# A first feed-forward pass in plain products, and Strassen's seven products on normalised rows, added up in one PSUM bank

## What is computed

```python
D_MODEL, FFN_DIM = 1024, 2816

def rmsnorm(x, g, eps=1e-6):
    return x * rsqrt(mean(x * x, axis=-1) + eps) * g

def swiglu(h, w1, w3, w2):
    return (silu(h @ w1) * (h @ w3)) @ w2

# in each of the two layers, after the mixer:
x = x + cross_attn(rmsnorm(x, g_cross), ...)      # ends in "@ wo", the output projection
x = x + swiglu(rmsnorm(x, g_ffn), w1, w3, w2)
```

## Time and profile before

| | us |
|---|---|
| median of 3 runs | 1830.64 |
| lowest and highest | 1827.59, 1831.19 |
| the profiled execution | 1831.32 |
| its span in the profile | 1829.5 |

### The profile page before, as it was taken

How to read it: one execution, slowest core, us unless ns; L and a number is a source line. 1 busy time by engine, 2 the same in 40 slices (tenths; PEclk the granted TensorE clock), 3 DMA queues, 4 the chain that set the end, 5 groups by cost and what they waited for, 6 DMA issues and landing times.

```text
span 1829.5 us, 28059 instructions
## 1 busy us (share of the span) xinstructions
PE 1723.5 (94%) x11264; PEld 1552.0 (85%) x11264; DVE 1196.1 (65%) x1918; ACT 683.0 (37%) x1229; POOL 512.0 (28%) x405
## 2 busy tenths in 40 slices
PE   7999998998899999999999999899979999999997
PEld 6566556987789999999999997699769999999997
DVE  3699857455894948586745135644669586668583
ACT  4021254354642515243442144533455243334241
POOL 3021101212632414233213132101175151415141
PEclk9999999999899999999999998999979999999999
DMA  7222420251204030303142224213221321222302
GB/s 249 98 85 83 117 93 7 106 216 42 75 30 139 27 129 18 127 30 110 41 139 49 92 70 175 98 47 139 93 92 38 105 69 46 102 69 75 123 19 86
DMA packets 39021, 162.32 MB, mean 89 GB/s; under 512 B 9368, under 2 KB 10008, under 8 KB 24944
## 3 DMA queue, kind: packets, MB, share of 16 engines
q1 hardware_dynamic: 30944, 121.97, 20.4%
q0 software_dynamic: 7952, 38.60, 5.9%
HBM read 149.87 MB, written 10.42 MB: 88 GB/s over the span
## 4 chain that ended last, share of the span: by engine, by line
PE 77%; DVE 13%; issue 4%; ACT 4%; POOL 1%; DMA 0%; SPq 0%; DVEq 0%; ACTq 0%; POOLq 0%
PE G L944 54%; PE S L944 13%; PE Q L944 9%; DVE w_split L2677 3%; DVE g_split L2708 1%; ACT work L1690 1%; ACT w_split L1690 1%; PE Q L1604 1%; DVE work L2733 1%; DVE w_split L2757 1%; ACT rstd L1690 1%; DVE work L2729 1%; POOL ring_split L795 1%; DVE work L2723 1%; ACT front L1690 1%
## 5 line engine op out<-in xcount | busy, mean ns | idle before, releaser
L1690 ACT ACTIVATE w_split<-ring 128x512 fp32r<-128x512 f32 (+2 forms) x232 | 157.0, 681 | 352.3 <-PE G L944 243.4
L944 PE MATMUL G<-ffn_rows,w_split 128*128 128x320 f32 x1680 | 252.9, 310 | 6.4 <-DVE work L2733 6.4
L944 PEld LDWEIGHTS G<-ffn_rows,w_split 128*128 128x128 f32 x1680 | 247.2, 188 | 9.7 <-DVE w_split L2677 9.7
L834 POOL TENSOR_TENSOR mkT<-ring 128x512 f32<-128x512 f32 x88 | 126.8, 1445 | 407.8 <-DVE w_split L2677 205.3
L944 PE MATMUL G<-front,ring 128*128 128x128 f32 (+2 forms) x832 | 223.6, 430 | 10.9 <-DMA ring<-in_w_mk 9.2
L944 PEld LDWEIGHTS G<-front,ring 128*128 128x128 f32 x832 | 133.2, 193 | 100.0 <-issue 95.8
L944 PE MATMUL G<-g_split,w_split 128*128 128x320 f32 x1344 | 203.4, 314 | 12.8 <-DVE w_split L2757 12.8
L944 PEld LDWEIGHTS G<-g_split,w_split 128*128 128x128 f32 x1344 | 201.8, 192 | 14.5 <-DVE w_split L2757 14.4
L944 PE MATMUL S<-ffn_rows,w_split 128*128 128x320 f32 x1152 | 177.8, 313 | 6.6 <-issue 6.2
L944 PEld LDWEIGHTS S<-ffn_rows,w_split 128*128 128x128 f32 x1152 | 173.2, 191 | 7.6 <-issue 6.7
L2757 DVE TENSOR_TENSOR w_split<-ring,w_split 128x512 fp32r<-128x512 f32 (+1 forms) x80 | 68.1, 862 | 148.6 <-ACT w_split L1690 148.6
(11 more groups left out here) (355 smaller groups left out, 2917.9 us busy)
## 6 DMA issues: line engine op xcount, KB each, us to landing
ring<-in_w_up SPq DMA_DIRECT2D x44, 1024.0 KB, 4.8
ring<-in_w_down SPq DMA_DIRECT2D x48, 256.0 KB, 2.6
ring<-in_w_down SPq DMA_DIRECT2D x32, 320.0 KB, 2.9
front<-in_mem_k POOLq DMA_DIRECT2D x8, 1024.0 KB, 7.1
front<-in_mem_v POOLq DMA_DIRECT2D x8, 1024.0 KB, 11.0
ring<-in_w_mk SPq DMA_DIRECT2D x4, 1024.0 KB, 6.0
ring<-in_w_mv SPq DMA_DIRECT2D x4, 1024.0 KB, 11.0
ring<-in_w_glu SPq DMA_DIRECT2D x4, 1024.0 KB, 8.5
```

Source lines behind the costliest of these rows:

```text
L834: nc.gpsimd.tensor_tensor(wsum[n], a, b, ALU.subtract).then_inc(sum_ready, 1)
L944: return nc.tensor.matmul(out, lhsT, rhs, start=start, stop=stop, **kw)
L1690: return nc.scalar.activation(*a, **k)
```

## The change

1. **Plain first pass.** `PASSES` becomes 4, 5, 5, 4, 4, and the four tiles of the first pass are plain products: 2 x 48 matmuls a tile instead of 84, on split rows `hs` (h_split), not normalised, as other projections use them. Their weight operands are 1024 wide, one for w1 and one for w3. VectorE multiplies by the norm twice a tile.
2. **Rows later.** During the plain tiles VectorE makes normalised rows (line 2685 of the new kernel) and their three sums (2696). The high and low parts of all seven row operands, each 128 x 1280, are made during the first down product, ahead of the down weights in both queues. The output projection keeps its natural order, and its rows take one split per block.
3. **Products in one bank.** In the other 18 tiles four of the seven products are added up in one PSUM bank. Between them ScalarE copies the bank out (`p1`, `u2`, `u3`), a fourth copy takes `p5`, and the next product into the bank waits for the copy. VectorE joins with five half-width operations, none by the norm.
4. **GpSimd** computes only the four weight differences of a tile; the row sums and its join are gone.
5. **PSUM and the down product.** All feed-forward work turns through four PSUM tiles. The first two down blocks both run n-1 of their n steps, then both their last one. At a pass's end the down weights of blocks 0 and 1 are split between the joins of the last tile. The first product after layer 0 waits for blocks of the last down product to be read.

The core of the diff:

```diff
-PASSES = (5, 5, 4, 4, 4)
+PASSES = (4, 5, 5, 4, 4)
+PLAIN = PASSES[0]
-WO = (0, 4, 1, 5, 2, 6, 3, 7)
...
-        UP = (("a11", 0, 0, 0, True), ("diff", 3, "b12-b22", 1, True), ("a", 1, 1, 0, False),
-              ("sums", 6, "b22-b12+b11", 1, False), ("sums", 5, "b12-b11", 2, True),
-              ("a", 2, "b21-b22+b12-b11", 3, True), ("sums", 4, 3, 2, False))
+        UP = ((0, 0), (5, "b12-b11"), (6, "b22-b12+b11"), (1, 1), (3, "b12-b22"), (4, 3), (2, "b21-b22+b12-b11"))
+        UP_BANK = (0, 2, 0, 1, 0, 2, 0)
...
+                def plain_tile(f, s):
+                    n = USE["up", f, s]
+                    tile_free(n)
+                    pe.wait_ge(op_low, operand(l, f, s) + 1)
+                    for k in range(KD):
+                        if f + s == 0:
+                            pe.wait_ge(applied, APPLIED[f"ffn{l}"] - KD + 1 + k)
+                        for wpart, xpart in ((0, 0), (0, 1), (1, 0)):
+                            for e in range(2):
+                                fr = slice(e * HT, (e + 1) * HT)
+                                m = mm(FT[l][n % 4][:, fr], ws[:, s, wpart, k * P:(k + 1) * P], hs[:, xpart, k, fr],
+                                       k == 0 and wpart + xpart == 0, k == KD - 1 and wpart == 1)
+                    m.then_inc(up_done, 1)
...
+                    if i < 2:
+                        tile_free(n + i)
+                    elif i in (2, 4, 6):
+                        pe.wait_ge(copied, 4 * q + (1, 3, 4)[i // 2 - 1])
+                    elif i == 5:
+                        pe.wait_ge(copied, 4 * q + 2)
+                    if f == PLAIN:
+                        pe.wait_ge(row_low, row_count(l, row))
...
                     down_part(p, 0, range(n - 1))
-                    down_part(p, 1, range(1))
+                    down_part(p, 1, range(n - 1))
                     down_part(p, 0, range(n - 1, n))
-                    down_part(p, 1, range(1, n))
+                    down_part(p, 1, range(n - 1, n))
...
+                    act.wait_ge(up_done, done + 1)
+                    if q:
+                        act.wait_ge(g_left, q)
+                    A(p1, y, ACT.Copy).then_inc(copied, 1)
                     up_high(f, 4)
+                    act.wait_ge(up_done, done + 2)
+                    if q:
+                        act.wait_ge(c22_ready, q)
+                    A(p5, z, ACT.Copy).then_inc(copied, 1)
                     up_high(f, 5)
+                    if f > PASS0[p]:
                         gate_high(f - 1)
+                    act.wait_ge(up_done, done + 3)
+                    A(u2, y, ACT.Copy).then_inc(copied, 1)
                     up_high(f, 6)
                     up_high(f, 7)
+                    act.wait_ge(up_done, done + 5)
+                    if f > PLAIN:
+                        act.wait_ge(g_raw, l * KH + f)
+                    A(u3, y, ACT.Copy).then_inc(copied, 1)
                     up_high(f, 8)
+                    act.wait_ge(c22_ready, q + 1)
+                    A(u3, u3, ACT.Silu).then_inc(silu, 1)
                     up_high(f, 9)
+                    if last:
+                        down_high(l, p, 0)
+                    act.wait_ge(c12_read, q + 1)
+                    A(u2, u2, ACT.Silu).then_inc(silu, 1)
                     up_high(f, 10)
...
+                        if p == 0 and j < 5:
+                            for row in (ROW_ORDER[0:1], ROW_ORDER[1:3], ROW_ORDER[3:5], ROW_ORDER[5:6], ROW_ORDER[6:])[j]:
+                                row_low_part(row)
+                            if j == 0:
+                                row_difference()
```

497 lines of the change are left out of this document (240 added, 257 removed).

## The result

The changed kernel takes 1772.86 us (1772.73 to 1774.0, four runs) against 1830.91 of the kernel before in the same comparison: a ratio of 0.9687, with a 95% interval of 0.967 to 0.9704. It is 58.0 us faster; the forecast was 44.7, so 1786.

A forecast was written before the change was run, and what follows sets the result against it. TensorE, busy 94%, was taken as the bound, VectorE second inside up tiles. Projection gains of 13.7 and 14.5 plus feed-forward gains of 7.1 and 9.4 made 44.7 off 1831.3, so 1786 us; 8-in-10 range 1767 to 1812.

The forecast's parts named there:

- everything hides: Rival: up tiles lose nothing (-12.8) and row splits overlap better (-6), giving 1767 us; chance 0.15.
- Projection: Output projection of both layers: the whole TensorE loss goes, 13.7 us in layer 0 and 14.5 in layer 1.
- the additions would still set the pace: Rival for the output projection: 4.1 us per block against TensorE's 3.5, 8 x 0.6 lost per layer, 1796; chance 0.08.
- Plain tiles: Four up tiles a layer take 96 matmuls instead of 84: 7.0 us more per layer, 14.1 each, no wait.
- Norm: The norm's four matmuls in the first up tile, counted as 1.9 us lost per layer.
- First down product: Row operands split ahead of the down weights: waits of 0.9, 2.2 and 0.8, sum 3.9 us, between 0 and 12.
- a bound of five: Clock: no low-clock stretch counted; bound one in half of the ten passes, 1.5 us each, 7.5.
- Other down starts: Later down products: block 2's weights wait for block 0's slot, 1.1 or 0.9 us each; sum 4.4 with 0.4 more.
- Up tiles: Strassen up tiles: VectorE needs 12.9 us against TensorE's 12.32, 0.6 lost in most, 6.4 per layer; bounds 0 and 26.
- small waits for ScalarE's copies: Sign to look for in Strassen tiles: TensorE's waits should name ScalarE's copies (work<-G, S, Q), small.
- The end of layer 0: Layer 0's last down product: TensorE waits 4.0 us for the next mixer's last rows instead of 0.7, 3.3 more.
- GpSimd holds VectorE for whole operations: Rival in the up tiles: each GpSimd difference stops VectorE for all its 1.55 us; 88 lost, 1861, slower; chance 0.05.

The follow-up runs named there:

- b_difference_first: Kernel before, with GpSimd's first row difference ahead of two low parts of the projection's weights: 1821.28 us against 1829.67, ratio 0.9959.
- a_old_interleave: Changed kernel with the first two down blocks interleaved as before (one step of block 1, block 0's last, block 1's rest): 1763.17 us, ratio 0.964.
- b_two_joins_less: Kernel before without two of the five half-width multiplications by the norm in each up tile (output lacks them): 1824.0 us, ratio 0.9968.
- a_norm_joins_back: Changed kernel with three half-width multiplications by the norm put back behind the additions of each Strassen tile: 1823.14 us, ratio 0.9964.
- a_spares_in_chain: Changed kernel with three unneeded half-width VectorE multiplications per Strassen tile, directly ahead of the join that frees the sixth product: 1807.09 us, ratio 0.9874.
- a_spares_in_gaps: Changed kernel with three unneeded half-width VectorE multiplications per Strassen tile, one each where VectorE stood idle: 1790.46 us, ratio 0.9785.

## Why the prediction was right, and where its sizes were off

The sign held, and so did the mechanisms of the projection, the plain tiles and the down products. The mechanism put forward for the up tiles did not, and half of the rival "everything hides" came true: the up tiles lose nothing, but the row splits still cost what was forecast. A loss below is taken from the starts of the rows against 0.1467 us a matmul, as in the forecast; the waits in brackets are smaller, since short pauses beside them are not in them.

Two rows of the changed kernel, a GpSimd sum and the low part of g beside it, show most of the delay that is left in a Strassen tile:

```profile
578.55 1.75 POOL L832 TENSOR_TENSOR mv<-ring,mkT 128x512 f32<-128x512 f32 x1
...
579.06 1.92 DVE L2720 TENSOR_TENSOR g_split<-work,g_split 128x640 fp32r<-128x640 f32 x1
```

Point by point:

- **Projection**, 13.7 and 14.5 forecast, 13.6 and 14.4 measured. b_difference_first shows that the chain through GpSimd made most of the first wait; the rest of the gain has the two causes named there. The rival that the additions would still set the pace (1796) falls: 180 matmuls in one row at 0.147 each.
- **Plain tiles**, 14.08 each, as forecast; 7.0 more a layer.
- **Norm**, 1.9 forecast, 1.0 measured. I took the four matmuls' time from a stretch where the clock was low (0.54 granted from 484.50 to 486.50); at clock 1.00 they take half.
- **First down product**, 3.9 forecast (0.9, 2.2, 0.8), 3.6 measured in layer 0 (0.8, 2.1, 0.7). Following the two queues found the right three waits and nearly their sizes. In layer 1 4.5 is lost: the second wait (1.79) was followed by 24 matmuls in 5.31 instead of 3.78, the low clock once, 1.5 us, and the third is gone. It is the only low stretch in ten down products, against a bound of five.
- **Other down starts**, 1.1 and 0.9 forecast for block 2, 1.1 and 0.9 measured (waits of 0.87 and 0.63). a_old_interleave shows that the cause was the slot of block 0, as worked out.
- **Up tiles**, 6.4 a layer forecast, nothing measured. This is the term that was mis-sized, and it is most of the error: 12.8 of the 13.9. The norm adds 1.8 and the down products take some 0.5 back, but for rounding. I put a tile of VectorE together as 8.0 of work, 2.5 of waits and handoffs and 2.4 of delay by GpSimd, 12.9 in all. The trace has 8.9 busy with GpSimd's delay in it. That delay is 1.4, not 2.4: 1.1 on the low part of g, which took 1.92 instead of 0.82 beside a GpSimd sum, and 0.3 on one low part of weights. The work in it is 7.5, not 8.0: low parts that last 0.69 start 0.60 apart. With both put right the sum is 11.4, which is 12.32 less the 0.9 to spare. The price per operation (0.6) was taken from a tile in which VectorE was full. In the emptier tile two of GpSimd's four (581.66 and 584.26) delay nothing: what runs beside them on VectorE had begun before, reads PSUM, or began in the sum's last 0.1 us. The step that failed is the adding up of VectorE's times against TensorE's 12.32; what decides is the chain of eleven steps with 0.9 to spare. The sign that the prediction gave for these tiles, small waits for ScalarE's copies, did not show either: there are none.
- **The end of layer 0**, 4.0 forecast up to the last rows, 3.9 measured, and the last low part ends 39.1 us after the product's start (39.2 forecast). But the forecast had one wait there; the trace spreads it, with 1.5 at 892.81, 1.1 at 905.15, 0.6 at 911.90 and 0.3 at each of two starts between.

The rival "GpSimd holds VectorE for whole operations" (1861) did not come, and the runs say why: 1.4 of delay where 4.6 was its threshold. It is real, though, as soon as operations meet. The Trainium skill ("SBUF — State Buffer", Who interferes with whom) says that a VectorE instruction with two SBUF inputs contends with a GpSimd instruction that reads SBUF, over a port pair that it calls an exclusive lock. The trace agrees on which are hit: operations with both inputs in SBUF, low parts among them (1.47, 1.59 and 1.29 for 0.5, 0.5 and 0.69). All 108 joins with a PSUM input took 475 to 493 ns in the changed kernel, and 476 to 493 with GpSimd's sums doubled. With the sums cut to 8 columns the low part takes 0.69 again. Only a part of GpSimd's 6.1 us reaches VectorE here; in the rows of this tile it depends on when the two start.

The miss in the up tiles could as well have gone the other way. The forecast had no measure of the margin, and the experiments show a slope behind it that is steep: three operations of 0.5 in the chain cost 34 us, ten more than with small sums.

## What to carry to other kernels

Where engines hand a tile to and fro, follow the longest chain of handoffs from one TensorE event to the next need and write down its margin; an engine's busy share says little (8.9 of 12.3 busy, and three operations of 0.5 cost 34 us in the chain and 18 spread over gaps). Count the delay by GpSimd from the operations that begin beside each other, not per GpSimd operation, and expect it to change when anything shifts. When a buffer slot is reused, put a whole block of work between its last reader and the need for what replaces it (18 or 24 matmuls were enough here, 6 were not).

## What the runs showed of the hardware

- TensorE's clock after a wait is not told by the wait's length alone. A wait of 1.78 in layer 0 (530.48) left 24 matmuls at 3.79, one of 1.79 in layer 1 (1389.02) was followed by 5.31. In before and b_two_joins_less the same wait of 2.18 left 240 matmuls at 35.48 or 37.00. Of eight waits of 1.9 in a_norm_joins_back six were followed by 36 matmuls in 7.04 and two by 36 in 5.52. What tells them apart stays open.
- An operation of VectorE with both inputs in SBUF that begins beside a GpSimd sum takes up to 1.1 us longer (1.92 for 0.82, 1.79 for 0.68), and one with an input in PSUM no longer (at most 493 ns). The loss can feed on itself: a delay moves the next operation beside the next sum, as the low part of 1.29 in a_spares_in_chain. In a_spares_in_gaps three operations of 0.5 cost up to 0.96 in a tile (13.28 for 12.32), though each was put into a gap of about 1 us.
